# First stage of a two-block transformer step: the modulation chunks come in pairs, part of the first key products and the gate weights move ahead of the first border

## The reference, cut to what matters

```
s_lat, s_ctx = silu(c), silu(c_ctx)
ml = split(s_lat @ w_ada[l] + b_ada[l], 6)      # shift, scale, ... of the latent stream
mc = split(s_ctx @ w_ada[l] + b_ada[l], 6)      # the same for the context stream
hl = rmsnorm(xl, norm_g[l, 0]) * (1 + ml[1]) + ml[0]
hc = rmsnorm(xc, norm_g[l, 0]) * (1 + mc[1]) + mc[0]
u  = [hc; hl] @ w_in[l]                          # queries, keys, values, gates, ... of three branches
lam = exp(sum(lq[0]*lq[1])) - exp(sum(lq[2]*lq[3])) + lam_init
```

## Time and profile before

| | us |
|---|---|
| median of 3 runs | 3083.03 (3082.73 to 3083.89) |
| span of the profiled execution | 3084.4 |
| end of ScalarE's last work in the first stage | 39.1 |
| first matmul of the second stage | 40.4 |
| query tile 2 begins on TensorE | 59.7 |

### The profile page before, as it was taken

One profiled execution on the slowest core, in us unless ns is written; L12 is line 12 of the kernel. 1 busy time (PEld: TensorE's weight loads), 2 busy tenths in 40 slices (PEclk: granted clock), 3 DMA queues, 4 the chain that ended last, 5 costly groups with the idle time before them and its releaser, 6 DMA issues. The chain is left out here.

```text
span 3084.4 us, 37774 instructions
## 1 busy us (share of the span) xinstructions
PE 2925.2 (95%) x14236; PEld 2261.5 (73%) x14236; DVE 1847.3 (60%) x3960; ACT 821.4 (27%) x1905; POOL 575.0 (19%) x565
## 2 busy tenths in 40 slices
PE   7999999999999999999999999999999999888777
PEld 3888877758888888887998878888888744443222
DVE  3556675367775677644445557534236777777774
ACT  2132254311002100012123430010033454444443
POOL 2223321010000000103112100000000354344342
PEclk9999999999999999999999999999999999999999
DMA  6212211154432554544322234568534899999997
GB/s 244 93 63 69 69 42 61 50 170 125 135 123 76 157 153 134 167 137 124 110 83 83 69 107 153 173 240 318 196 120 138 310 420 420 420 421 420 421 416 323
DMA packets 278084, 582.23 MB, mean 189 GB/s; under 512 B 11720, under 2 KB 228936, under 8 KB 241552
## 3 DMA queue, kind: packets, MB, share of 16 engines
q0 software_dynamic: 51504, 338.98, 28.1%
q1 hardware_dynamic: 226400, 240.84, 24.1%
HBM read 578.70 MB, written 1.08 MB: 188 GB/s over the span
## 5 line engine op out<-in xcount | busy, mean ns | idle before, releaser
L4302 PE MATMUL banks<-weight_ring,work 128*128 128x512 f32 x512 | 249.3, 611 | 50.8 <-ACT work L4128 49.7
L4302 PE MATMUL banks<-work 128*128 128x512 f32 x512 | 250.7, 612 | 41.0 <-ACT work L4128 40.0
L436 DVE CUSTOM_DVE_ANT_0 work<-work 128x1024 f32<-128x1024 f32 x176 | 210.2, 1228 | 99.4 <-ACT branches L2830 46.9
L2608 PE MATMUL banks<-normed,weight_ring 128*128 128x256 f32 x1088 | 240.1, 384 | 6.7 <-ACT normed L2808 3.8
L2608 PEld LDWEIGHTS banks<-normed,weight_ring 128*128 128x128 f32 x1088 | 209.7, 193 | 36.5 <-ACT normed L2808 4.2
L3945 DVE CUSTOM_DVE_ANT_0 weight_ring<-weight_ring,branches 128x1024 f32<-128x1024 f32 x128 | 156.8, 1225 | 86.8 <-DMA weight_ring<-experts,branches 84.9
L4302 PEld LDWEIGHTS banks<-weight_ring,work 128*128 128x128 f32 x512 | 87.6, 189 | 161.2 <-ACT work L4128 98.2
L3945 DVE CUSTOM_DVE_ANT_0 work<-work,branches 128x1024 f32<-128x1024 f32 x128 | 156.8, 1226 | 77.4 <-DMA work<-experts,branches 72.0
L4302 PEld LDWEIGHTS banks<-work 128*128 128x128 f32 x512 | 87.6, 189 | 153.5 <-ACT work L4128 91.2
L406 POOL DMA_DIRECT2D work<-ada_turned x96 | 51.1, 533 | 772.3 <-DVEq L442 772.3
L3910 POOL DMA_INDIRECT weight_ring<-experts,branches x128 | 137.8, 1077 | 195.8 <-PE banks L4302 182.4
(11 more groups left out here) (653 smaller groups left out, 5595.4 us busy)
## 6 DMA issues: line engine op xcount, KB each, us to landing
weight_ring<-w_in SPq DMA_DIRECT2D x98, 1024.0 KB, 5.3
weight_ring<-w_ffn_in SPq DMA_DIRECT2D x44, 1024.0 KB, 5.2
work<-ada_turned POOLq DMA_DIRECT2D x80, 512.0 KB, 3.8
work<-ada_turned POOLq DMA_DIRECT2D x16, 1536.0 KB, 8.9
weight_ring<-w_ffn_out SPq DMA_DIRECT2D x18, 1024.0 KB, 5.4
weight_ring<-w_out SPq DMA_DIRECT2D x12, 1024.0 KB, 5.4
weight_ring<-w_br_ml SPq DMA_DIRECT2D x8, 1024.0 KB, 5.1
weight_ring<-w_br_da SPq DMA_DIRECT2D x8, 1024.0 KB, 5.2
```

The lines of the kernel that those rows point to most:

```text
L436: last = dve.tensor_tensor_reduce(out=out, in0=slot[:, t, :], in1=self.rows[:, row, :], scale=1.0, scalar=0.0, op0=ALU.mult, op1=ALU.add, ...
L2608: ins = pe.matmul(bank(i)[:, 0:NLAT], w[:, k - at, half * P:(half + 1) * P], source[:, k, lat], start=k == 0, stop=k == total - 1)
L4302: last = pe.matmul(c.banks[2 * t + half][:], diag[:, r, :], vrows[r][:, half * 512:(half + 1) * 512], start=e == t * H * K, stop=e == (t + ...
```

## The change

In `start` the chunks come in four pairs: shift chunk and scale chunk of the same two channel tiles, 2 MB together, `fetch` of ring slot 0 after the first pair. One pair is multiplied in 16 passes over 512 columns, copied out once and turned into four tiles. VectorE adds the squares in pairs, so that four instead of eight products with ones are made. VectorE multiplies each tile with `rstd` (`level`), then, per pair, forms shift and scale for both conditions, and applies both at once: ScalarE to the context half (`activation` with `scale` and `bias`), VectorE to the latent half (`tensor_scalar`). As soon as tile `k` is done, TensorE multiplies it with the first two key column tiles (`keys(k)`, banks 6 and 7), for six of the eight `k`; the second stage does only the last two. The gate weights are loaded in the first stage, and GpSimd spreads them. Between `level` and `tensor_scalar` VectorE has three small operations per pair (shift plus bias; scale plus bias; scale plus one, times `norm_g`), each on two tiles and both conditions. In `branches` of layer 0 the load of the gate weights, `gate_apart` and the wait for it fall away.

```
-            for i in range(chunks):
-                sp.dma_start(held[i], a["w_ada_first"][first_tile[i] // tiles]).then_inc(c.chunk_loaded[i], 16)
-            fetch(c, sp, following[0:1])
+            for i in range(pairs):
+                for s, chunk in enumerate((pairs + i, i)):
+                    sp.dma_start(held[i][:, s], a["w_ada_first"][chunk]).then_inc(c.chunk_loaded[i], 16)
+                if i == 0:
+                    fetch(c, sp, following[0:1])
+            sp.dma_start(wg, w_in[:, :, COL_GATE:COL_GATE + 16]).then_inc(c.gate_loaded, 16)
...
+            for k in range(0, KT, 2):
+                pe.wait_ge(c.paired, k // 2 + 1)
+                last = pe.matmul(sums, c.constant("ones"), c.h[:, k, :], start=k == 0, stop=k == KT - 2)
...
+            def keys(k):
+                if k == 0:
+                    pe.wait_ge(c.ahead[0], 16)
+                pe.wait_ge(c.scaled, k + 1)
+                pe.wait_ge(c.moved, k + 1)
+                for half in range(2):
+                    pe.matmul(c.banks[6 + half][:], c.ring[:, 0, k, half * P:(half + 1) * P], c.h[:, k, :], start=k == 0, stop=False)
...
+            conditions(0); turn(0); keys(0); conditions(1); keys(1); turn(1); conditions(2); keys(2); turn(2)
+            keys(3); conditions(3); keys(4); turn(3); keys(5)          # one call to a line in the code
...
+            def level(i):
+                for k in (2 * i, 2 * i + 1):
+                    dve.tensor_tensor(c.h[:, k, :], c.x[:, k, :], rstd, ALU.mult).then_inc(c.ml_leveled, 1)
+            level(0)
+            for i in range(pairs):
+                dve.wait_ge(c.turned, i + 1)
...
+                for k in (2 * i, 2 * i + 1):
+                    dve.wait_ge(c.ml_leveled, k + 1)
+                    part = stream(k, 1)
+                    dve.tensor_scalar(part, part, c.modA[:, 1, k:k + 1], c.mod[:, k, 1:2], ALU.mult, ALU.add).then_inc(c.scaled, 1)
+                if i + 1 < pairs:
+                    level(i + 1)
...
 -            sp.dma_start(wg, w_in[:, :, COL_GATE:COL_GATE + 16]).then_inc(c.gate_loaded, 16)
+            if not full:
+                sp.dma_start(wg, w_in[:, :, COL_GATE:COL_GATE + 16]).then_inc(c.gate_loaded, 16)
```

More of the change, by code:

```diff
@@ L59 @@
 START_TILES = ADA_FIRST
+START_KEYS = 6
 ADA_SLOTS, ADA_GROUP = 2, 3
@@ L451, in tiles, with gate_weights, start @@
             yield
-def start(c, a, following):
-    conditions, streams = (0, 1), ((0, NCTX), (NCTX, T))
+def gate_weights(c):
+    scratch = c.mg[:].rearrange("p k t -> p (k t)")
+    return (scratch[:, 0:KT * 16].rearrange("p (k x) -> p k x", k=KT),
+            scratch[:, KT * 16:KT * 16 + KT * 32].rearrange("p (k x) -> p k x", k=KT))
+def start(c, a, w_in, following):
+    streams = ((0, NCTX), (NCTX, T))
     chunks = START_TILES * P // CHUNK
+    pairs = chunks // 2
     tiles = CHUNK // P
     flat = c.big[:].rearrange("p k t -> p (k t)")
-    held = [flat[:, i * KT * CHUNK:(i + 1) * KT * CHUNK].rearrange("p (k n) -> p k n", k=KT) for i in range(6)]
-    held += [c.mg[:, 4 * i:4 * i + 4, :].rearrange("p k t -> p (k t)").rearrange("p (k n) -> p k n", k=KT) for i in range(2)]
+    size = 2 * KT * CHUNK
+    held = [flat[:, i * size:(i + 1) * size] for i in range(3)] + [c.work[:, 4096:4096 + size]]
+    held = [x.rearrange("p (two k n) -> p two k n", two=2, k=KT) for x in held]
     wide = c.work[:, 0:KT * 32].rearrange("p (k m) -> p k m", k=KT)
@@ L464, in start, with turned, stream @@
     mean, rstd = c.work[:, 1024:1024 + T], c.work[:, 1536:1536 + T]
-    partial = c.work[:, 2048:2048 + chunks * CHUNK].rearrange("p (i n) -> p i n", i=chunks)
+    partial = c.work[:, 2048:2048 + pairs * 2 * CHUNK].rearrange("p (i n) -> p i n", i=pairs)
     early = CST["upper"][0]
[L467 to L473, removed]
+    wg, wg_apart = gate_weights(c)
+    PICK, MEAN = 1, 2
+    sums = c.banks[5]
+    def turned(pair):
+        return c.banks[2 + pair][:, 0:4 * tiles].rearrange("p (s t a) -> p s t a", s=2, a=2)
+    def stream(k, condition):
+        return c.h[:, k, slice(*streams[condition])]
     with c.stage() as block:
@@ L489, in _ @@
                 c.ahead_n[s] += 1
+        @block.gpsimd
+        def _(pool):
+            pool.memset(wg_apart, 0.0).then_inc(c.gate_cleared, 1)
+            pool.wait_ge(c.gate_cleared, 1)
+            pool.wait_ge(c.gate_loaded, 16)
+            pool.tensor_copy(wg_apart[:, :, 0:16], wg).then_inc(c.gate_apart, 1)
+            pool.wait_ge(c.gate_apart, 1)
         @block.tensor
@@ L493, in _, with conditions @@
             pe.wait_ge(c.side_loaded, 32)
-            for k in range(KT):
-                pe.wait_ge(c.squared, k + 1)
-                last = pe.matmul(c.banks[7][:], c.constant("ones"), c.h[:, k, :], start=k == 0, stop=k == KT - 1)
+            for k in range(0, KT, 2):
+                pe.wait_ge(c.paired, k // 2 + 1)
+                last = pe.matmul(sums, c.constant("ones"), c.h[:, k, :], start=k == 0, stop=k == KT - 2)
             last.then_inc(c.pe_out, 1)
[L499 to L503, removed]
+            def conditions(i):
+                pe.wait_ge(c.chunk_loaded[i], 32)
+                if i >= 2:
+                    pe.wait_ge(c.drained, i - 1)
                 for step in range(2):
                     for group in range(4):
-                        last = pe.matmul(c.banks[i % 4][32 * group:32 * group + 32, 0:CHUNK], wide[:, 2 * group + step, :],
-                                         held[i][:, 2 * group + step, :], start=step == 0, stop=step == 1)
+                        last = pe.matmul(c.banks[i % 2][32 * group:32 * group + 32, :], wide[:, 2 * group + step, :],
+                                         held[i][:, :, 2 * group + step, :], start=step == 0, stop=step == 1)
                 last.then_inc(c.product, 1)
@@ L512, in turn @@
                 pe.wait_ge(c.drained, i + 1)
[L513 to L516, removed]
+                for j in range(2 * tiles):
+                    last = pe.matmul(c.banks[2 + i][:, 2 * j:2 * j + 2], partial[:, i, j * P:(j + 1) * P], pick, start=True, stop=True)
                 last.then_inc(c.turned, 1)
+            def keys(k):
[5 more added lines that the diff above has]
+                    pe.matmul(c.banks[6 + half][:], c.ring[:, 0, k, half * P:(half + 1) * P], c.h[:, k, :], start=k == 0, stop=False)
             pe.wait_ge(c.conditioned, 1)
             pe.wait_ge(c.vec_out, PICK)
[L521 to L525, removed]
+            conditions(0)
+            turn(0)
+            keys(0)
+            conditions(1)
+            keys(1)
+            turn(1)
+            conditions(2)
+            keys(2)
+            turn(2)
+            keys(3)
+            conditions(3)
+            keys(4)
+            turn(3)
+            keys(5)
         @block.scalar
@@ L538, in copy @@
                 act.wait_ge(c.product, i + 1)
-                act.activation(partial[:, i, :], c.banks[i % 4][:, 0:CHUNK], ACT.Copy).then_inc(c.drained, 1)
-            for i in range(chunks // 2):
-                copy(i)
+                act.activation(partial[:, i, :], c.banks[i % 2], ACT.Copy).then_inc(c.drained, 1)
+            copy(0)
             act.wait_ge(c.vec_out, MEAN)
             act.activation(rstd, mean, ACT.Sqrt).then_inc(c.rooted, 1)
[L545 to L552, removed]
+            for i in range(pairs):
+                act.wait_ge(c.merged, 2 * (i + 1))
+                for k in (2 * i, 2 * i + 1):
+                    act.wait_ge(c.ml_leveled, k + 1)
+                    part = stream(k, 0)
+                    act.activation(part, part, ACT.Identity, bias=c.mod[:, k, 0:1], scale=c.modA[:, 0, k:k + 1]).then_inc(c.moved, 1)
+                if i + 1 < pairs:
+                    copy(i + 1)
         @block.vector
@@ L561, in _ @@
             dve.sem_inc(c.vec_out, 1)
+            for k in range(0, KT, 2):
+                dve.wait_ge(c.squared, k + 2)
+                dve.tensor_tensor(c.h[:, k, :], c.h[:, k, :], c.h[:, k + 1, :], ALU.add).then_inc(c.paired, 1)
             dve.wait_ge(c.pe_out, 1)
-            chain(dve.tensor_scalar(mean, c.banks[7][:], 1.0 / D, EPS, ALU.mult, ALU.add))
+            chain(dve.tensor_scalar(mean, sums, 1.0 / D, EPS, ALU.mult, ALU.add))
             chain(dve.reciprocal(mean, mean))
             dve.sem_inc(c.vec_out, 1)
-            def turned(lo, condition):
-                return turned_bank(lo)[:, 2 * lo:2 * lo + 2 * KT].rearrange("p (t a) -> p t a", a=2)[:, :, condition]
@@ L569, in _ @@
[L569 to L576, removed]
@@ L577, in _ @@
-            chain.wait()
-            dve.wait_ge(c.rooted, 1)
[L579 to L586, removed]
-                                  ).then_inc(c.merged, 1)
@@ L588, in _, with both @@
[L588 to L593, removed]
+            dve.wait_ge(c.rooted, 1)
+            def both(x):
+                return x.unsqueeze(2).to_broadcast([P, tiles, 2])
+            def level(i):
+                for k in (2 * i, 2 * i + 1):
```

(35 more changed lines are left out.)

1 line of the change is left out of this document (removed).

## The result

The changed kernel takes 3088.69 us in the median of 18 runs, the kernel before 3083.16 in as many on the same chip: a ratio of 1.0017, 95% interval 1.001 to 1.0025, so 3.1 to 7.7 us slower. One run of the changed kernel here (5068.73 us, granted clock 0.556) and one of the kernel before on a second chip (5355.95 us) are far slower than all others and stand in no ratio or mean. On that second chip the ratio was 1.0012 (1.0003 to 1.0022). The profiled execution has a span of 3088.1 us, 3.7 more than that of before.

The account below looks back on a forecast made before the run. TensorE was taken to bound the kernel through the moment query tile 2 begins: border 6.2 us later, 5.2 taken back behind it, so 1.0 later and a median of 3084.0 us; range from the no-wait case (3076.2) up to 3088.

Parts of the forecast that it names:

- no-wait case: Behind the border: lambdas through before TensorE needs them, tile 2 starts 6.3 us behind it; 6.8 us less, 3076.2; chance 0.16.
- the idle time from 20 to 24: First stage: TensorE, done with the first conditions and turn by about 20, idles some 4 us until the first key product.
- border: Between first and second stage: the second stage's first matmul comes at 46.6 instead of 40.4, 6.2 us later.
- What bounds, and the mark: First 60 us: gain or loss is the shift of query tile 2's start, 59.7 before; TensorE is busy without a break behind.
- Sums and first key product: First stage: TensorE starts sums at 10.0, they are out at 16.7, and the first key product can start at 24.0.
- Products to the border: From 24.0: 18.9 us of TensorE work at full clock plus 2.4 for half clock, ending at 45.3; then 1.3 of border.
- After the border: Second stage start: gate total waits for ScalarE's copy, ready 10.9 us behind the border; TensorE idles 5.6, half clock costs 2.3.
- the mean of the row: Lambda products behind the border at 0.95 us each wherever they stand, copy ready at 7.7; sum 3.2 us lower; not taken.
- the GpSimd ends: Lambda products behind the border each wait for the GpSimd operation in hand, the last at 9.5 us, copy ready at 10.9; taken.
- Sum: Whole kernel: border 6.2 us later, 5.2 taken back, query tile 2 at 60.7, 1.0 later; median 3084.0.
- The clock holds: TensorE keeps full clock through one or both idle gaps: 2.4 or 4.7 us less, 3079.3 to 3081.6; chance 0.18.
- The clock stays low: First-stage products: half clock not lifted by the mixed passes; up to 16.5 us later, 3100; slower case given chance 0.08.

Follow-up runs that it names:

- e1: The changed kernel with the lambda products, sums and exponentials put behind the gate chain: 3079.39 us, ratio 0.9982 to the kernel before.
- a2: The changed kernel again, unchanged, eleven runs on the second chip: 3087.89 us, ratio 1.0012 to the kernel before.
- b2: The kernel before again, unchanged, eleven runs on the second chip: 3083.79 us, ratio 0.9996 to the kernel before.
- e6: The changed kernel with six unused filler products between key tile 1 and the gate total: 3082.61 us, ratio 0.9994 to the kernel before.
- e4: The changed kernel with four unused filler products between the first turn and the first early key product: 3082.93 us, ratio 0.9996 to the kernel before.

## Why the prediction was wrong

It said 3084.0 us, 1.0 more than before, with a range from the no-wait case (3076.2) up to 3088; it is 5.5 more by the medians, and 0.7 above the range. The signs that it named came: the idle time from 20 to 24, the half clock in part of what follows, L1432 (L1391 before) over 7 us, over 5 us of idle time before the gate total; the border came 0.6 us after its 46.6. The mechanism is right; the sum is not.

- *What bounds, and the mark.* Right: what the traces show of a difference, beside the low clock, lies ahead of query tile 2 or in the half clock that reaches into it, and TensorE passes it on to the values.
- *Sums and first key product.* Right: 24.0 forecast, 24.03 measured, with some luck. TensorE started at 10.63 and not at 10.0, since the squares came 0.5 later, and its eight passes took 6.1 us and not 6.7. That this stretch ran at half speed is read from the distance of the passes (0.85 us against 0.43), in the earlier trace rows as here; the column PEclk shows 1.00 in it (10.63 to 15.57).
- *Products to the border.* 18.9 us at full clock forecast, 19.2 found (21.78 from 24.03 to 45.81, less 2.6): a `keys` takes 1.82 to 1.90 and not 1.72, a `turn` 0.81 to 0.88 and not 1.0. Clock 2.4 against 2.6; border 1.3 against 1.4. In sum 47.2 where 46.6 stood; over four traces the border moves by 7.1 and not 6.2.
- *After the border.* The wait is right to 0.1 us: copy of the gate operand ready 10.9 behind the border forecast, gate total at 58.17 - 47.22 = 10.95. Forecast were ends of the products at 4.75, 7.1 (and one more in the gap) and 9.5 us behind the border; they ended at 4.8, 7.1, 7.3 and 9.5. The choice between the mean of the row and the GpSimd ends was decided as taken: 6.95 us under `mix_tokens`, 0.63 alone (e1). The rule of the Trainium skill that was weighed there ("SBUF — State Buffer", section "Who interferes with whom": the later of the two waits for the other to finish) agrees with both numbers. The clock cost 2.5 to 2.6 where 2.3 stood, so that query tile 2 has an effective start 14.5 us behind the border (89.16 less 27.47, its way to the values in e1, less 47.22) and not 14.1.
- *Sum.* This is the step that failed. Its two terms, border 6.2 later and 5.2 taken back, are 7.1 and 4.9 in the means of four traces: 2.1 later, not 1.0, mostly by the three small misses above (products, clock, effective start). These alone would have given 3085.1. The larger miss is a term that the sum put at nothing: behind query tile 2 "the waits that I looked at move along". They do, but not all executions have the same low clock there: 24 to 41 us of it in the eight traces, worth 8 us. Single runs of the kernel before lie between 3078.6 and 3086.4 on the first chip. Medians scatter less: 3083.2, 3084.2 and 3085.0 on three chips. That the sum set one execution's 59.7 beside a median of three did no harm: the values begin at 87.16 in that trace and at 87.2 in the mean of four. Its step from a span of 3084.4 to the median 3083.0 mixed two measures (every run on record takes about 1.8 us more than its own span), which cancels in the difference.
- *What stays open.* 2.1 us in the traces, 3.1 to 7.7 by the first interval, 0.9 to 6.8 by the second. The second holds the 2.1, the first doesn't. Two of the traced executions are far from typical: a2's was the shortest of its eleven (3084.22), b2's the longest (3088.57). The record has a mean granted clock for every run on the second chip: 0.9911 in the mean of the changed kernel's eleven runs and in that of 37 of the kernel before, at mean times of 3087.8 and 3084.1. So over the whole execution the changed kernel meets no more low clock than the kernel before, and 3.7 us of difference remain. But it meets less of it ahead of 90 us (13.7 us in each of four traces, 16.2 in the mean of four before), so equal means leave it about 2.6 us more behind, worth 1.3: with the 2.1 that makes 3.4 of the 3.7. This is an estimate, since a run's clock is on record to three decimals only. For the first chip, where 3.4 of the 5.5 us are unexplained, the runs of the kernel before have no clock on record, and the cause stays open there.
- *Rivals.* "The clock holds" and "no wait" did not happen, but e6, e4 and e1 made them happen. "No wait" was priced 6.3 us from border to query tile 2 against 14.1, 7.8 in all: e1 measured 6.42 (52.71 - 46.29) and 8.0. "The clock stays low" did not happen: it came back after 5.2 us.

## What to carry to other kernels

Before work is moved ahead of a border, look at what was hidden behind it: here some 10 us of TensorE work (the 12 key products) covered a chain through VectorE (held up by GpSimd) and ScalarE that nobody needed so early, and the move exposed it. Put such a chain behind the one that the next engine waits for (e1), and count a gap like the two here (3.7 and 5.2 us) on TensorE twice: once as idle time and once as half clock after it (2.6 us each). Where executions of one kernel spread by several us, compare more than one trace of each, with the low clock beside the time.

## What the runs showed of the hardware that was not expected

- A VectorE operation on a few columns can last as long as GpSimd's operation beside it: 2.26 us for 128 x 8 (L1677), 6.95 for four of 128 x 64, against 0.63 for the same four alone.
- Filler products whose result nobody reads won time: 3.5 us of them in a gap made the way from the first key product to the border 2.5 us shorter (e4), since the dense work after it ran at 1.00 instead of 0.50; 5.3 us of them in the second gap won 2.5 us behind the border (e6).
- The spread between the executions of these two kernels is, within 1 us, the low clock in places where nothing was changed: 23.9 us of it against 41.0 in two executions of the kernel before, and spans of 2990.9 and 2999.0 after the values begin.
